# Two transformer blocks, first attention: low parts of fourteen gate panels on GpSimd instead of VectorE

## The chip, the cores and the metric

The kernel runs on one core of a Trainium2 chip. The metric is the device time of one execution in microseconds (us); lower is better. The core has TensorE (PE, matmuls, with its weight loads shown as PEld), VectorE (DVE), ScalarE (ACT), GpSimd (POOL) and the queue engine SyncE (SP). They run their own instruction streams and wait for each other through semaphores.

## The reference, cut to what matters

Two transformer blocks run one after the other on 512 tokens of width 1024, all in float32. The first begins with an attention of 8 "fox" heads and 8 "NSA" heads. Each NSA head is the sum of three softmax attentions: over compressed keys, selected keys and a window. Beside the attention, two gates of 1024 columns are made from the same normed input and weight the two attentions afterwards:

```python
h = rms_norm(x, g_attn)
z = h @ w_in                        # q, k, v, ..., g_a, g_b
s = q @ k^T * scale + bias          # per head; causal
p = softmax(s); o = p @ v
merged = sigmoid(g_a) * (o_fox @ w_br_fox) + sigmoid(g_b) * (o_nsa @ w_br_nsa)
x = x + merged @ w_out
```

The rest (a feed-forward part, then the second block with modulation, attention, a depthwise convolution and another feed-forward part) is untouched by the change.

## The kernel before, in words

**Panels.** Every weight matrix is cut into panels of 128x1024 numbers (512 KB). A panel goes through a ring of four slots: SP loads it into `raw`, ACT rounds it into `w_hi` (`panel_hi`, lines 666 to 670), VectorE subtracts `w_hi` from `raw` into `w_lo` (`panel_lo`, lines 1170 to 1175), and PE multiplies. A float32 product is three matmuls: high by high, high by low and low by high. Semaphores count in panel order: `hi_ready` and `lo_ready` say how many panels are split, `used` how many PE has finished. The split of a panel is made two panels ahead (`AHEAD = 2`).

**The attention.** It is a list of 32 steps, `inst`: 8 fox heads (steps 0 to 7), then for each of 8 NSA heads a compressed (cmp), a selected (slc) and a window (win) step. A step s of the PE stream (from line 2262 on) makes the scores of s (`qk`, line 2194), the transposed probabilities of step s-2 (`turn_p`, line 2214) and their product with the values (`pv`, lines 2239 and 2240). Between them it fills in matmuls of the 16 gate panels (`gate_fill`, lines 2253 to 2255), up to six places a step. Tables written out when the program is built (`GATE_FILL`, `GATE_ENDS`) say which gate piece goes where. The gate panels end in steps 1, 2, 4, 6, 8, 10, 12, 15, 17, 19, 21, 24, 26, 28, 30 and 33.

**VectorE in a step**, in this order: scores of step s with bias and row maximum (`score`, line 1340; t = 0 and 1, later 2 and 3), the sum of a head (`o_add`, 1394), the low parts of the transposed probabilities (`lo_turn`, 1378), the scaled gate output (`gate_out`, 1403), the softmax factor (1351, 1355) and the scaling of the probabilities of step s-1 (`normalize_tiles`, 1368, a tensor_scalar from and to SBUF). If a gate panel ended in this step, the low part of the panel two further on follows (`panel_lo`), and only then the low part of a finished head (`o_lo`, 1386) and the scores of the next step. PE's third score piece of a step waits for the first `score` of that step, and its transposes wait for the scaling.

**ScalarE in a step**: exponentials (763), high parts of transposed probabilities (774), `panel_hi` (669), the high part of a head (`o_hi`, 786), and for fox steps the four bias tiles of the next head (`fox_bias`, 755), for all of which the first score waits.

**GpSimd during the attention** issues transfers only. The loop at line 519 runs over 16 bias loads, n = 0 to 15: wait for the buffer (the fox bias of head n-2, or the scores of a later step), issue the bias transfer (533), and for n < 8 also wait for PE and issue the four key transfers of a head (`fox_keys`, 516) and one store of bias rows (537). Its other arithmetic comes later: squares of the context (547 to 553) and seven convolution taps (573 to 578).

Of the kernel before, what the change touches and what calls it, by code (L numbers as in the profile page):

```python
# [16 lines left out]
F32 = mybir.dt.float32  # L17
F32R = mybir.dt.float32r
ALU = mybir.AluOpType
# [27 lines left out]
RING = 4  # L47
AHEAD = 2
# [37 lines left out]
BASE, PANELS = {}, 0  # L86
# [6 lines left out]
def build(nc, a, out):  # L93
# [7 lines left out]
    def place(name, shape, dt, at=None):  # L101

        n = int(np.prod(shape[1:]))
        n = (n + 7) // 8 * 8
        if at is None:
            at = mark["at"]
            mark["at"] += n
        assert at + n <= room, (name, at, n, room)
        return nc.alloc_sbuf_tensor_at(name, list(shape), dt, offset=base0 + 4 * at)

    raw = place("raw", [P, RING, 8, P], F32)
    w_hi = place("w_hi", [P, RING, 8, P], F32R)
    w_lo = place("w_lo", [P, RING, 8, P], F32R, 0)
# [166 lines left out]
    def sem(name):  # L280
        if name not in sems:
            sems[name] = nc.alloc_semaphore(name)
        return sems[name]
# [3 lines left out]
    hi_ready = sem("panel_hi_ready")  # L287
    lo_ready = sem("panel_lo_ready")
# [35 lines left out]
    NI = len(inst)  # L324
# [84 lines left out]
    def gates_ended(s):  # L409
        return [g for (r, n), g in sorted(GATE_ENDS.items()) if r == s]  # L410
# [73 lines left out]
    def _(gp):  # L484
# [21 lines left out]
        def fox_keys(h):  # L506
# [7 lines left out]
            for m, k in enumerate((k_hi, k_lo)):  # L514
                for half in HALF:
                    gp.dma_start(kd[h % 2][half, m, :], k[HALF[h % 2], h // 2, :]).then_inc(sem(f"keys_loaded_{h % 2}"), 16)

        gp.wait_ge(sem("rows_stored"), 16)
        for n in range(16):
            if n == 8:  # L520
                gp.wait_ge(sem("rel_stored"), 16 * 8)
            if n >= 2:
                m = n - 2
                if m < 8:
                    gp.wait_ge(sem("fox_bias"), 4 * (m + 1))
                else:
                    gp.wait_ge(sem("scored"), 4 * (8 + 3 * (m - 8) + 3))
            if n < 8:
                src = bass.AP(tensor=scratch_c.tensor, offset=n * T, ap=[[0, P], [1, T]])
            else:  # L530
                head = (n - 8) // 2 + 4 * ((n - 8) % 2)
                src = bass.AP(tensor=scratch_r.tensor, offset=head * P * 640 + 127, ap=[[639, P], [1, T]])
            gp.dma_start(bias[:, n % 2, :], src).then_inc(sem(f"bias_loaded_{n % 2}"), 16)
            if n < 8:
                fox_keys(n)
                gp.wait_ge(sem("rel_rows"), 2)
                gp.dma_start(scratch_r[:, n * REL_ROWS:(n + 1) * REL_ROWS, :],
                             r8[:].unsqueeze(1).to_broadcast([8, REL_ROWS, 640])).then_inc(sem("rel_stored"), 16)
        gp.wait_ge(sem("qk_done"), NT * 8)
        gp.dma_start(cst[:, C_EARLY:C_ALL], a["consts"][:, C_EARLY:C_ALL]).then_inc(in_c2, 16)  # L540
        gp.wait_ge(used, done(BASE["branch"] + 7))
# [604 lines left out]
    def _(dve):  # L1146
# [24 lines left out]
        def panel_lo(n, also=0):  # L1171

            dve.wait_ge(hi_ready, n + 1)
            dve.tensor_tensor(w_lo[:, n % RING], raw[:, n % RING], w_hi[:, n % RING].bitcast(F32), ALU.subtract)\  # L1174
               .then_inc(lo_ready, 1 + also)
# [234 lines left out]
        for s in range(NI + 3):  # L1410
            score(s, 0)
            score(s, 1)
            if s >= 3 and head_end(s - 3):
                o_add(s - 3)
            lo_turn(s - 2, 0)
            gate_at(s, 0)
            score(s, 2)
            score(s, 3)
            if s == 0:
                proj_low("n3")  # L1420
                panel_lo(BASE["gate"] + 1)
            if s == 1:
                dve.wait_ge(sem("vc_hi_done"), 1)
                dve.tensor_tensor(vcs[:, :, 1, :], ps[0:CW, 7, P:2 * P].rearrange("p (g d) -> p g d", g=2),
                                  vcs[:, :, 0, :].bitcast(F32), ALU.subtract)\
                   .then_inc(sem("vc_lo_done"), 1)
            gate_at(s, 1)
            lo_turn(s - 2, 1)
            gate_at(s, 2)
            normalize_factor(s - 1)  # L1430
            lo_turn(s - 2, 2)
            gate_at(s, 3)
            normalize_tiles(s - 1, (0, 1))
            lo_turn(s - 2, 3)
            if s < NI + 2:
                gate_at(s, 4, 5)
            normalize_tiles(s - 1, (2, 3))
            for g in gates_ended(s) if s < NI + 2 else []:
                panel_lo(BASE["gate"] + g + AHEAD)
            if s >= 3 and head_end(s - 3):  # L1440
                o_lo(s - 3)
        for g in gates_ended(NI + 2):
            panel_lo(BASE["gate"] + g + AHEAD)
            gate_out(g)
        dve.wait_ge(bank_free, BASE["branch"] + 2)
# [156 lines left out]
        for c in range(4):  # L1602
            for m in range(8):
                n = BASE[f"ff1_{c}"] + m
# [10 lines left out]
            for m in range(8):  # L1615
                n = BASE[f"ff2_{c}"] + m
# [4 lines left out]
                if c == 0 and m == 0:  # L1621
                    g = vec[:, V_AT["g_final"]:V_AT["g_final"] + 8]
# [19 lines left out]
        for m in range(8):  # L1642
            n = BASE["ff2_3"] + m
# [303 lines left out]
        for c in range(3):  # L1947
            g = f"up_{c}"
# [710 lines left out]
```

## Time and profile before

| | before |
|---|---|
| median of 3 runs | 1712.98 us (1711.72 to 1714.76) |
| the profiled execution's own time | 1713.54 us |
| its span in the trace | 1711.8 us |
| busy: PE, DVE, ACT, POOL | 95%, 65%, 42%, 10% of the span |
| granted PE clock, mean | 0.986 of full speed |

The profiled execution is 0.56 us above the median, and 1.74 us of it lie outside the span. The attention with its gate panels fills some 165 us to 406 us of the span. A busy PE is not one at its peak: matmuls overlap, and their ends are modelled. In a row of the timeline the bracket says how long the engine was idle before it and who released it; "x4" means that four instructions of one kind are merged, with their common length.

### The profile page before, as it was taken

How to read it: one execution, taken by the hardware profiler on the slowest of the kernel's cores; microseconds unless marked ns; L12 is line 12 of the kernel's file. 1: busy time of each engine (PE TensorE's matmuls, PEld its weight loads, DVE VectorE, ACT ScalarE, POOL GpSimd, SP SyncE). 2: the span in 40 equal slices, each digit the busy share in tenths (PEclk: the TensorE clock that was granted, in tenths of full speed). 3: DMA queues.
4: the chain of work that ended last, by engine and by line, in shares of the span. 5: the costliest groups of instructions: out<-in, count | busy, mean ns of one | idle time of the engine just before them, and what ended most of it. 6: DMA issues, size and time to landing. Idle time of an engine off the chain costs nothing.

```text
span 1711.8 us, 21979 instructions
## 1 busy us (share of the span) xinstructions
PE 1629.8 (95%) x7956; PEld 1345.3 (79%) x7956; DVE 1110.3 (65%) x1700; ACT 716.3 (42%) x1232; POOL 164.7 (10%) x187
## 2 busy tenths in 40 slices
PE   7999889998999999999989999999899899999997
PEld 5877777776788888888867787888778888888886
DVE  6764787776577666663677479998665644444456
ACT  5353875555443232322443244444534432232233
POOL 0012400000120000000002980000000000000000
PEclk9999999999999999999999999999999999999999
DMA  4346921112535554531314221221232233332333
GB/s 160 120 123 175 190 69 50 46 49 61 219 113 178 203 202 168 207 135 63 98 37 136 87 73 44 63 62 50 92 123 76 86 98 98 94 92 97 99 98 99
DMA packets 49969, 185.43 MB, mean 108 GB/s; under 512 B 6928, under 2 KB 9232, under 8 KB 47456
## 3 DMA queue, kind: packets, MB, share of 16 engines
q1 hardware_dynamic: 39600, 136.76, 25.0%
q0 software_dynamic: 10288, 47.60, 9.8%
q8 instruction: 51, 0.84, 0.2%
q14 instruction: 30, 0.25, 0.0%
HBM read 172.23 MB, written 6.85 MB: 105 GB/s over the span
## 4 chain that ended last, share of the span: by engine, by line
PE 77%; DVE 12%; ACT 5%; issue 3%; DMA 2%; SPq 0%; ACTq 0%; DVEq 0%
PE ps L2004 17%; PE ps L2005 16%; PE ps L2006 16%; PE ps L2066 2%; PE ps L2067 2%; PE ps L2068 2%; ACT w_hi L669 1%; PE ps L2253 1%; PE ps L2214 1%; PE ps L2255 1%; PE ps L2421 1%; PE ps L2419 1%; PE ps L2254 1%; PE ps L2420 1%; DMA raw<-in_panels 1%
## 5 line engine op out<-in xcount | busy, mean ns | idle before, releaser
L2004 PE MATMUL ps<-h_hi,w_hi 128*128 128x512 f32 x832 | 329.2, 396 | 9.5 <-DVE h_lo L1672 3.7
L2005 PE MATMUL ps<-h_lo,w_hi 128*128 128x512 f32 x832 | 324.0, 389 | 0.0
L2006 PE MATMUL ps<-h_hi,w_lo 128*128 128x512 f32 x832 | 323.9, 389 | 0.0
L1174 DVE TENSOR_TENSOR w_lo<-raw,w_hi 128x1024 fp32r<-128x1024 f32 x181 | 228.4, 1264 | 119.0 <-ACT w_hi L669 93.0
L602 ACT ACTIVATE w_hi<-raw 128x1024 fp32r<-128x1024 f32 x125 | 131.4, 1052 | 168.3 <-DMA raw<-in_panels 162.3
L2004 PEld LDWEIGHTS ps<-h_hi,w_hi 128*128 128x128 f32 x832 | 156.2, 188 | 49.8 <-DVE h_lo L1672 5.8
L2005 PEld LDWEIGHTS ps<-h_lo,w_hi 128*128 128x128 f32 x832 | 156.2, 188 | 33.4 <-issue 1.9
L2006 PEld LDWEIGHTS ps<-h_hi,w_lo 128*128 128x128 f32 x832 | 156.2, 188 | 32.9
L2004 PE MATMUL ps<-f_hi,w_hi 128*128 128x512 f32 x408 | 164.8, 404 | 0.0
L2005 PE MATMUL ps<-f_lo,w_hi 128*128 128x512 f32 x408 | 159.1, 390 | 0.0
L2006 PE MATMUL ps<-f_hi,w_lo 128*128 128x512 f32 x408 | 159.0, 390 | 0.0
L669 ACT ACTIVATE w_hi<-raw 128x1024 fp32r<-128x1024 f32 x122 | 127.9, 1051 | 43.1 <-DMA raw<-in_panels 42.8
L2066 PE MATMUL ps<-h_hi,w_hi 128*128 128x512 f32 x184 | 75.4, 410 | 18.1 <-DVE w_lo L1174 18.1
L1159 DVE TENSOR_TENSOR w_lo<-raw,w_hi 128x1024 fp32r<-128x1024 f32 x70 | 85.6, 1223 | 8.5 <-DVE tmp_s L1959 4.5
L2006 PEld LDWEIGHTS ps<-f_hi,w_lo 128*128 128x128 f32 x408 | 76.6, 188 | 16.2
L2004 PEld LDWEIGHTS ps<-f_hi,w_hi 128*128 128x128 f32 x408 | 76.8, 188 | 13.8 <-issue 0.2
L2005 PEld LDWEIGHTS ps<-f_lo,w_hi 128*128 128x128 f32 x408 | 76.9, 188 | 13.6 <-issue 0.2
L774 ACT ACTIVATE pt_hi<-ps 128x512 fp32r<-128x512 f32 (+4 forms) x104 | 46.4, 447 | 72.5 <-PE ps L2214 71.8
L2067 PE MATMUL ps<-h_lo,w_hi 128*128 128x512 f32 x184 | 73.9, 402 | 0.0
L880 ACT ACTIVATE tmp_v<-tmp_s 128x512 f32<-128x512 f32 x32 | 20.2, 633 | 128.1 <-DVE tmp_s L1608 128.1
L1378 DVE TENSOR_TENSOR pt_lo<-ps,pt_hi 128x512 fp32r<-128x512 f32 (+4 forms) x104 | 52.4, 504 | 32.9 <-ACT pt_hi L774 30.6
L2068 PE MATMUL ps<-h_hi,w_lo 128*128 128x512 f32 x184 | 73.4, 399 | 0.0
(421 smaller groups left out, 3347.3 us busy)
## 6 DMA issues: line engine op xcount, KB each, us to landing
raw<-in_panels SPq DMA_DIRECT2D x252, 512.0 KB, 3.5
wm<-in_w_mod POOLq DMA_DIRECT2D x16, 1536.0 KB, 8.3
scratch_r<-r POOLq DMA_DIRECT2D x8, 320.0 KB, 10.6
bias<-scratch_c POOLq DMA_DIRECT2D x8, 256.0 KB, 10.4
kd<-k_hi POOLq DMA_DIRECT2D x16, 128.0 KB, 4.4
kd<-k_lo POOLq DMA_DIRECT2D x16, 128.0 KB, 6.8
bias<-scratch_r POOLq DMA_DIRECT2D x8, 256.0 KB, 3.1
X<-in_x POOLq DMA_DIRECT2D x1, 2048.0 KB, 9.7
```

The costliest lines, as they stand in the source:

```text
L602: act.activation(w_hi[:, slot], raw[:, slot], ACT.Copy).then_inc(hi_ready, 1)
L669: act.activation(w_hi[:, n % RING], raw[:, n % RING], ACT.Copy).then_inc(hi_ready, 1)
L774: act.activation(pt_hi[0:rows, at:at + w], ps[0:rows, 4 + r % 2, 0:w], ACT.Copy).then_inc(sem("pt_hi_done"), 1)
L1159: dve.tensor_tensor(w_lo[:, slot], raw[:, slot], w_hi[:, slot].bitcast(F32), ALU.subtract).then_inc(lo_ready, 1)
L1174: dve.tensor_tensor(w_lo[:, n % RING], raw[:, n % RING], w_hi[:, n % RING].bitcast(F32), ALU.subtract)\
L1378: dve.tensor_tensor(pt_lo[0:rows, at:at + w], ps[0:rows, 4 + r % 2, 0:w], pt_hi[0:rows, at:at + w].bitcast(F32), ALU.subtract).then_inc(se ...
L2004: pe.matmul(out, w_hi[:, u, b, :], hi[:, k, :N], start=start, stop=False)
L2005: pe.matmul(out, w_hi[:, u, b, :], lo[:, k, :N], start=False, stop=False)
L2006: ins = pe.matmul(out, w_lo[:, u, b, :], hi[:, k, :N], start=False, stop=stop)
L2066: pe.matmul(out, hi, h_hi[:, k, :], start=k == 0, stop=False, skip_group_check=True)
L2067: pe.matmul(out, hi, h_lo[:, k, :], start=False, stop=False, skip_group_check=True)
L2068: ins = pe.matmul(out, lo, h_hi[:, k, :], start=False, stop=k == KT - 1, skip_group_check=True)
```

## The change

GpSimd makes the low parts of gate panels 2 to 15, in its own stream, in place of VectorE. Before each bias load n it makes those panels whose gate ended before step `BIAS_STEP[n]`. That puts panel 2 before load 4, panel 3 before load 5, panel 4 before load 7, panel 5 before load 9, panel 6 before load 10, panels 7 and 8 before load 11, panel 9 before load 12, panel 10 before load 13, panels 11 and 12 before load 14, panel 13 before load 15, and panels 14 and 15 after load 15, ahead of the load of the rotary constants. VectorE keeps the panels around them and waits for GpSimd's count before the next one it makes itself.

```diff
+        def gate_low(g):
+
+            n = BASE["gate"] + g + AHEAD
+            gp.wait_ge(hi_ready, n + 1)
+            gp.wait_ge(lo_ready, n)
+            gp.tensor_tensor(w_lo[:, n % RING], raw[:, n % RING], w_hi[:, n % RING].bitcast(F32), ALU.subtract)\
+              .then_inc(lo_ready, 1)
+
+        BIAS_STEP = [n - 2 if n < 10 else 10 + 3 * (n - 10) for n in range(16)]
+        LOWS = [(s, g) for s in range(NI + 2) for g in gates_ended(s) if g + AHEAD < 16]
+
+        def gate_lows(until):
+
+            while LOWS and LOWS[0][0] < until:
+                gate_low(LOWS.pop(0)[1])
+
         gp.wait_ge(sem("rows_stored"), 16)
         for n in range(16):
+            gate_lows(BIAS_STEP[n])
...
+        gate_lows(NI + 2)
         gp.wait_ge(sem("qk_done"), NT * 8)
...
             for g in gates_ended(s) if s < NI + 2 else []:
-                panel_lo(BASE["gate"] + g + AHEAD)
+                if g + AHEAD >= 16:
+                    dve.wait_ge(lo_ready, BASE["gate"] + g + AHEAD)
+                    panel_lo(BASE["gate"] + g + AHEAD)
...
         for g in gates_ended(NI + 2):
+            dve.wait_ge(lo_ready, BASE["gate"] + g + AHEAD)
             panel_lo(BASE["gate"] + g + AHEAD)
```

## Rows read from the trace of the kernel before

**Rows 1.** The page: the chain by engine, and one kind of transfer with its landing time.

```profile
PE 77%; DVE 12%; ACT 5%; issue 3%; DMA 2%; SPq 0%; ACTq 0%; DVEq 0%
...
bias<-scratch_c POOLq DMA_DIRECT2D x8, 256.0 KB, 10.4
```

**Rows 2.** Windows, attention: length, busy PE, PEld, DVE, ACT, POOL, clock, DMA, GB/s.

```profile
165.00:390.00 225.00, 207.24 (x1113) 163.88 (x1113) 175.23 (x565) 150.83 (x426) 24.67 (x45) 0.97 0.36 84
```

**Rows 3.** Waits of PE, 165 to 390 us: total, times, longest.

```profile
PE ps L2194 <- DVE neg_max L1340: 3.6, 5, 0.9
```

**Rows 4.** Groups of DVE by line, 175 to 375 us: the moved instruction.

```profile
L1174 DVE TENSOR_TENSOR w_lo<-raw,w_hi 128x1024 fp32r<-128x1024 f32 x14 | 17.1, 1219 | 2.6 <-ACT w_hi L669 2.6
```

**Rows 5.** Timeline of steps 5, 9 and 13: start, length, instruction, idle before.

```profile
205.05 1.21 DVE L1174 TENSOR_TENSOR w_lo<-raw,w_hi 128x1024 fp32r<-128x1024 f32 x1
...
207.27 0.29 DVE L1340 CUSTOM_DVE_ANT_0 sb<-ps,sb 128x128 f32<-128x128 f32 x1 [0.28 <-ACT sb L755]
...
237.76 1.22 DVE L1174 TENSOR_TENSOR w_lo<-raw,w_hi 128x1024 fp32r<-128x1024 f32 x1
...
239.01 0.69 DVE L1386 TENSOR_TENSOR qs<-o_sum,qs 64x512 fp32r<-64x512 f32 x1
...
240.08 0.45 PE L2194 MATMUL ps<-kn_hi,nqs 128*128 128x384 f32 x1 [0.55 <-DVE neg_max L1340]
...
266.22 1.23 DVE L1174 TENSOR_TENSOR w_lo<-raw,w_hi 128x1024 fp32r<-128x1024 f32 x1 [0.66 <-ACT w_hi L669]
...
267.12 0.60 PE L2211 MATMUL ps<-cst,p_cmp 128*32 128x128 f32 x4
267.71 0.44 PE L2194 MATMUL ps<-kn_hi,nqs 128*128 128x384 f32 x1
```

**Rows 6.** Instructions of lines 547 and 578: shortest, median, longest in ns.

```profile
L547 POOL TENSOR_TENSOR c_sq<-x_ctx x8: 607/839/1595, 465.6 to 481.2; 128x256 f32<-128x256 f32 x8
L547 POOLq MODIFY_POOL_CONFIG  x2: 42/42/42, 454.3 to 454.3; - x2
...
L578 POOL TENSOR_TENSOR conv<-conv,conv_p x24: 1267/1292/1988, 934.7 to 1019.0; 128x512 f32<-128x512 f32 x24
```

**Rows 7.** Timeline of POOL and DVE where both compute, later in the kernel.

```profile
467.69 0.61 POOL L547 TENSOR_TENSOR c_sq<-x_ctx 128x256 f32<-128x256 f32 x1
467.98 0.60 DVE L1467 COPY sq_acc<-tmp_s 128x512 f32<-128x512 f32 x1
...
968.32 1.29 POOL L578 TENSOR_TENSOR conv<-conv,conv_p 128x512 f32<-128x512 f32 x1
968.45 2.23 DVE L1174 TENSOR_TENSOR w_lo<-raw,w_hi 128x1024 fp32r<-128x1024 f32 x1 [4.69 <-ACT w_hi L669]
```

**Rows 8.** Instructions of line 1485: the same copy with GpSimd quiet.

```profile
L1485 DVE COPY sq_acc<-tmp_s x2: 417/417/417, 1293.7 to 1672.9; 128x512 f32<-128x512 f32 x2
```

**Rows 9.** Timeline around the scaling (L1368) of steps 2, 10 and 28.

```profile
187.03 1.05 ACT L669 ACTIVATE w_hi<-raw 128x1024 fp32r<-128x1024 f32 x1
...
188.50 0.81 DVE L1368 TENSOR_SCALAR sb<-sb,factor 128x384 f32<-128x384 f32 x2
...
250.23 0.54 POOL L533 DMA_DIRECT2D bias<-scratch_r  x1 [25.26 <-DVE neg_max L1340]
...
250.85 1.27 DVE L1368 TENSOR_SCALAR sb<-sb,factor 128x128 f32<-128x128 f32 x4
...
252.18 0.66 PE L2214 MATMUL ps<-cst,sb 128*128 128x128 f32 x4 [0.58 <-DVE sb L1368]
...
368.89 1.04 ACT L669 ACTIVATE w_hi<-raw 128x1024 fp32r<-128x1024 f32 x1
...
370.40 1.27 DVE L1368 TENSOR_SCALAR sb<-sb,factor 128x128 f32<-128x128 f32 x4
```

**Rows 10.** Timeline: bias load 4 is issued, and ScalarE begins to use it.

```profile
180.82 0.57 POOL L533 DMA_DIRECT2D bias<-scratch_c  x1 [1.24 <-ACT sb L755]
...
196.26 1.91 ACT L755 ACTIVATE sb<-bias,c_q 128x128 f32<-128x128 f32 x4
```

## The prediction

> **What bounds the kernel now.** I read the page first, then the stages, then the waits, then single steps. The chain on the page is 77% PE and 12% DVE [rows 1]: the kernel is bound by TensorE, and VectorE matters only where PE waits for it. In the stretch of the attention where the fourteen moved instructions lie, PE is busy for 207.2 of 225 us and VectorE for 175.2, with GpSimd at 24.7 [rows 2]. So no more than about 18 us of PE idle time can be had there, from whatever cause. The moved work is fourteen subtractions of 1.219 us, 17.1 us in all [rows 4]. That is not the gain. The gain is only what PE waits right behind them, and the wait in question is that of the third score piece for the first score: 3.6 us in five cases [rows 3], one of which (step 1) belongs to a panel that VectorE keeps.
>
> **What is removed.** I went through the places one by one.
> - Steps 5 and 7 (fox). The w_lo begins at 205.05 and ends at 206.26, yet the first score starts at 207.27 and was released by ScalarE's bias tiles, after 0.28 us of idleness [rows 5]. Without w_lo it starts at the same time. Gain: nothing.
> - Step 9. After w_lo comes the head's low part (0.69 us) and then the score, and PE has 0.55 us of idle time in front of its score piece [rows 5]. This would come back, if nothing took its place.
> - Four steps like 13 (the others are 16, 22 and 25). VectorE waits 0.66 us for w_hi and works 1.23 us, then scores. PE starts four transposes at 267.12 and the next score piece only at 267.71, right as the first score (some 0.28 us, behind w_lo) must end [rows 5]. No bracket marks a wait, but part of these 0.59 us is one: bounds nothing and 0.59, and I take 0.35. Gain: 4 x 0.35 = 1.4 us.
> - In the remaining places (steps 2, 11, 18, 20, 27, 29) PE does not wait behind w_lo.
>
> **What is added: the length on GpSimd.** The trace has no 128x1024 tensor_tensor on POOL. A 128x256 one takes at least 0.607 us and a 128x512 one 1.267 us, median 1.292 [rows 6]. Another 512 columns at the same slope give an estimate of 1.29 + 2 x 0.68 = 2.65 us. Bounds: 2.4 us (four times the smallest) and 4.0 us (twice the slowest 512-column one). I take 2.65. As to PE this is hidden: a low part is made one whole gate panel ahead, ten or more us, so PE will not wait for it. VectorE's new wait for the count before the two panels it keeps (steps 31 and 33) costs nothing for the same reason: the last moved panel belongs to step 28.
>
> **What is added: the two engines get in each other's way.** This is the term that decides. At 967 to 971 us a w_lo that takes 1.22 us alone takes 2.23 us; it began at 968.45 under a POOL tensor_tensor that ended at 969.61 [rows 7, 4]. The 1.01 us extra are the rest of that instruction (1.16) less 0.15. A copy from SBUF to SBUF takes 0.417 us alone and 0.602 us when it begins 0.32 us before the end of a POOL instruction [rows 7, 8]: again the rest, less 0.14. So a VectorE instruction of either kind simply stands until GpSimd's is over. The page "SBUF — State Buffer" of the Trainium skill has this as a rule (section "Who interferes with whom"): a VectorE instruction with two SBUF inputs, or in a mode that uses two ports, fully blocks against a GpSimd instruction that reads SBUF, whoever starts second. The trace agrees, with the two cases above.
>
> What is caught during 2.65 us after w_hi is done?
> - Step 3 (w_hi of step 2). It is done at 188.08; the scaling (two instructions, 0.81 us) starts at 188.50 [rows 9]. It would be held until 188.08 + 2.65 - 0.14 = 190.6 and end at 191.4, against 189.3. The score came after w_lo, at 190.4; now at 191.4. PE waits for both. Cost +1.0 us.
> - Steps 5 and 7. GpSimd gets the port when the scaling ends, by 205.05, and holds it to 207.7. The head's low part (two SBUF inputs, 0.69 us) is then held to 207.55 and ends at 208.25, where the score used to start at 207.27 [rows 5]. +1.0 us each, 2.0.
> - Step 9. From 237.76 to 240.4; the low part ends at 240.95 and not at 239.70 [rows 5]. +1.25 us, instead of the gain of 0.55.
> - Step 29. w_hi is done at 369.93, 0.47 us before the four scalings at 370.40 [rows 9]; GpSimd has nothing else to do. They are held for 2.65 - 0.47 - 0.14 = 2.0 us, and PE's transposes wait for them (as in step 11, 0.58 us already [rows 9]). +2.0 us.
> - Steps 11 and 20, the same pattern, but here GpSimd is issuing a bias transfer until 250.77, and the scaling starts at 250.85 [rows 9]. Which comes first can't be told from 0.08 us. If GpSimd: 2.65 - 0.08 - 0.14 = 2.4 us each. If VectorE: nothing, as its work goes back to back. I count half, 2.4 us for the two.
> - Steps 2, 13, 16, 18, 22, 25 and 27: behind w_hi come scores and low parts with one operand in PSUM. Nothing is caught; in 18 and 27 only if GpSimd slips in between two scalings.
>
> **GpSimd's own queue.** Behind each subtraction stands a bias load. Load 4 is issued at 180.82, lands 10.4 us later and is first used at 196.26 [rows 1, 10]: 5.0 us of room, of which the subtraction takes at most 1.5 to 2. The later loads are further ahead. The load of the rotary constants moves behind panel 15; it is used in the second block. Cost nothing. If this cover went, ScalarE's bias tiles would be late, then the first score, then PE.
>
> **The sum.** -1.4 + 1.0 + 2.0 + 1.25 + 2.0 + 2.4 = +7.25 us. The profiled execution took 1713.54, so 1720.8; its median stands 0.56 lower, so 1720.2. Nothing downstream gives it back: after the attention PE is the bound again, and panels are loaded as PE uses them.
>
> **Rivals.**
> 1. The blocking is as weak for these forms as if it weren't there. For it speaks that no row shows a tensor_scalar beside a POOL tensor_tensor; against it the copy. Then step 9 and the four like 13 gain 0.55 + 1.4 = 2.0 us, and 0.4 in step 3: 2.4 us, 1710.6. It decides once the instructions of steps 3, 5, 7 and 9 are held for less than about 0.5 us each instead of some 2. With every wait behind the first scores gone (3.6 us of rows 3 and 1.4) it would be at most 5 us, 1708.
> 2. Part of the cost is absorbed: VectorE has 17 us less to do, and where PE is held for the scaling, later waits of the step shrink. With steps 11 and 20 won by VectorE and a quarter of the rest absorbed: 0.75 x 4.85 = +3.6, 1716.6.
> 3. GpSimd's first arithmetic must be set up. MODIFY_POOL_CONFIG comes at 454.3 and the first tensor_tensor at 465.6, behind a transfer that covers the gap [rows 6], so its price lies between nothing and 11.3 us. It would now come ahead of panel 2, and with GpSimd free 1.24 us before 180.82 [rows 10] load 4 would land at 179.6 + 11.3 + 2.65 + 10.4 = 204.0, which is 7.7 us late; step 3's collision (1.0) would be avoided. That gives up to 6.7 us more, 1726.9. The page "GPSIMD Engine Reference" (section "Instruction dispatch") puts a first load at some 6 us; by this estimate load 4 would be 2.4 us late and the time 1721.6. No run here shows it.
> 4. A clock drop. PE's granted clock is 0.97 over the stage [rows 2]; longer stalls might add a stretch at 1.2 GHz or take one away, some 2 us either way. This widens the range only.
>
> **How the numbers follow.** Forecast (blocking, sum between 4.85 and 9.65 us) 0.58; rival 1, 0.13; rival 2, 0.16; rival 3, 0.13. A measurement of this kernel can tell about 0.2%, 3.4 us. Faster by more needs rival 1 at its end: 0.06. Within 3.4 us: the rest of rival 1 and half of rival 2, 0.17. Slower: 0.77. The range reaches from 1711.5 (rival 1 short of its centre) to 1727 (rival 3 at its bound, or the full sum with drops).
>
> **What would show it.** Right: fourteen POOL subtractions near 2.65 us; L1368 and L1386 rows longer by up to 2.5 us in steps 2 to 10, 19 and 28; longer waits of L2214 and L2194; no change in slc and win steps but a small gain. Wrong: L1368 and L1386 at their old lengths; PE waiting for w_lo; ScalarE's L755 waiting for a bias transfer.

## The result, and the profile after

The changed kernel takes 1730.25 us (median of 5 runs, 1727.54 to 1731.13) against 1713.3 for the kernel before (5 runs): ratio 1.0097, 95% interval 1.0083 to 1.011. It is slower, by more than twice what I had forecast (1720.2), and it lies above my range, which ended at 1727. The profiled execution took 1731.13 us.

In the changed file the lines have moved: the scaling is L1386 (before L1368), the head's low part L1404 (L1386), the product that makes the scaling's factors L1373 (L1355), the scores L1358 (L1340), the transposes of PE L2235 (L2214), its score pieces L2215 (L2194), VectorE's w_lo L1192 (L1174). The subtractions on GpSimd are L523, the bias loads L550.

The page of the changed kernel: span, busy time, chain by engine, the bias loads.

```profile
span 1729.3 us, 21995 instructions
...
PE 1634.3 (95%) x7956; PEld 1349.0 (78%) x7956; DVE 1116.1 (65%) x1686; ACT 716.3 (41%) x1232; POOL 198.6 (11%) x201
...
PE 75%; DVE 14%; ACT 5%; issue 4%; DMA 2%; SPq 0%; ACTq 0%; DVEq 0%
...
bias<-scratch_c POOLq DMA_DIRECT2D x8, 256.0 KB, 9.2
```

The chain gave two per cent from PE to VectorE [rows 1 for before]. The bias loads land in 9.2 us, not later than before (10.4), so by this figure nothing in that queue suffered. Now PE's waits for the whole attention, changed kernel, 167 to 407 us: total, times, longest.

```profile
PE ps L2235 <- DVE sb L1386: 14.3, 8, 2.9
...
PE ps L2215 <- DVE neg_max L1358: 4.1, 4, 1.6
```

The wait of rows 3 (3.6 us, for the first scores) is still there, though w_lo is gone from before them; it now comes with the held low part of steps 5 and 7, as below at 212.91. Beside it stands one that is much larger: PE's transposes wait for the scaling, 14.3 us in eight cases. The same view of the kernel before, 165 to 390 us, has it at its old size:

```profile
PE ps L2214 <- DVE sb L1368: 2.4, 4, 0.7
```

The subtractions themselves, line 523: shortest, median, longest in ns, first and last start.

```profile
L523 POOL TENSOR_TENSOR w_lo<-raw,w_hi x14: 2349/2398/2660, 181.1 to 382.9; 128x1024 fp32r<-128x1024 f32 x14
L523 POOLq MODIFY_POOL_CONFIG  x2: 74/74/74, 180.9 to 181.0; - x2
```

They take 2.40 us, my lower bound, where I took 2.65. The configuration takes 74 ns and the first subtraction begins at 181.05, right behind it.

The timeline of the changed kernel around four collisions, in steps 3, 5, 9 and 11: start, length, instruction, idle time before.

```profile
190.40 2.35 POOL L523 TENSOR_TENSOR w_lo<-raw,w_hi 128x1024 fp32r<-128x1024 f32 x1 [1.19 <-ACT w_hi L687]
190.74 2.62 DVE L1386 TENSOR_SCALAR sb<-sb,factor 128x384 f32<-128x384 f32 x2
193.41 1.11 PE L2235 MATMUL ps<-cst,sb 128*128 128x128 f32 x4 [2.46 <-DVE sb L1386]
...
209.32 2.66 POOL L523 TENSOR_TENSOR w_lo<-raw,w_hi 128x1024 fp32r<-128x1024 f32 x1 [1.05 <-ACT w_hi L687]
209.93 2.60 DVE L1404 TENSOR_TENSOR qs<-o_sum,qs 64x512 fp32r<-64x512 f32 x1 [0.19 <-ACT qs L804]
212.91 0.44 PE L2215 MATMUL ps<-kd,qs 128*128 128x384 f32 x1 [1.55 <-DVE neg_max L1358]
...
242.95 2.95 DVE L1386 TENSOR_SCALAR sb<-sb,factor 128x384 f32<-128x384 f32 x2
243.24 2.37 POOL L523 TENSOR_TENSOR w_lo<-raw,w_hi 128x1024 fp32r<-128x1024 f32 x1 [12.99 <-ACT w_hi L687]
...
257.57 2.54 DVE L1373 TENSOR_TENSOR factor<-factor,gate_t 128x4 f32<-128x4 f32 x1
257.71 2.37 POOL L523 TENSOR_TENSOR w_lo<-raw,w_hi 128x1024 fp32r<-128x1024 f32 x1
260.15 1.27 DVE L1386 TENSOR_SCALAR sb<-sb,factor 128x128 f32<-128x128 f32 x4
261.48 1.10 PE L2235 MATMUL ps<-cst,sb 128*128 128x128 f32 x4 [2.94 <-DVE sb L1386]
```

Read each pair together. At 190.74 two scalings that take 0.81 us take 2.62, until 0.6 us after the subtraction ends. At 209.93 the head's low part (0.69 us alone) takes 2.60. So far this is what I had described. At 242.95 the first of two scalings had already begun when GpSimd came, and the pair still took 2.95 us: GpSimd got in between the two (the second one, 128x512, begins at 243.28 and takes 2.62 us). And at 257.57 it is not the scaling that is held but the product before it, four numbers wide, which takes 0.166 us in the kernel before (next row). Its record begins 0.14 us before that of the subtraction.

```profile
L1355 DVE TENSOR_TENSOR factor<-factor,gate_t x24: 165/166/171, 243.4 to 395.1; 128x4 f32<-128x4 f32 x24
```

In step 2 the lead is longer still. The last scaling of that step, seen by itself (180.6 to 182 us, one engine at a time):

```profile
180.44 3.35 DVE L1386 TENSOR_SCALAR sb<-sb,factor 128x512 f32<-128x512 f32 x1
...
181.05 2.44 POOL L523 TENSOR_TENSOR w_lo<-raw,w_hi 128x1024 fp32r<-128x1024 f32 x1
```

Alone it takes 0.47 us, so it would have ended at 180.91, 0.14 us before the subtraction's record begins. It did not.

The clock is the second part. Windows of the kernel before and then of the changed one: stretch, length, busy PE, PEld, DVE, ACT, POOL, granted clock, DMA share, GB/s.

```profile
165.00:195.00 30.00, 26.08 (x147) 21.48 (x148) 20.12 (x59) 21.57 (x52) 12.36 (x24) 1.00 0.94 192
...
370.00:400.00 30.00, 27.06 (x136) 20.66 (x137) 22.46 (x73) 17.04 (x51) 0.00 (x0) 0.94 0.11 35
```

```profile
165.00:195.00 30.00, 23.73 (x131) 19.28 (x130) 21.22 (x51) 20.73 (x49) 15.35 (x21) 0.97 0.95 196
...
370.00:400.00 30.00, 26.04 (x136) 21.02 (x134) 22.18 (x67) 13.92 (x44) 4.64 (x3) 0.89 0.13 38
```

PE's clock falls to its lower level, 1.2 GHz, at 193.3, as the long wait of step 3 ends, and at 384.4, within the one that ends at 386.6. Before, it did not fall in step 3, and in step 29 it was low for 3.4 us where it now is for 6.8.

### The profile page after: what moved, and what is told of

Read it like the earlier page. It is cut to its first block, busy times and chain, and to the rows that moved or that the text cites. A ratio compares the mean times of both kernels' runs of the same rounds, so it can differ in the third digit from the quotient of the medians.

```text
span 1729.3 us, 21995 instructions
## 1 busy us (share of the span) xinstructions
PE 1634.3 (95%) x7956; PEld 1349.0 (78%) x7956; DVE 1116.1 (65%) x1686; ACT 716.3 (41%) x1232; POOL 198.6 (11%) x201
## 4 chain that ended last, share of the span: by engine, by line
PE 75%; DVE 14%; ACT 5%; issue 4%; DMA 2%; SPq 0%; ACTq 0%; DVEq 0%
PE ps L2025 17%; PE ps L2027 16%; PE ps L2026 16%; PE ps L2087 2%; PE ps L2089 2%; PE ps L2088 2%; PE ps L2235 2%; ACT w_hi L687 1%; PE ps L2274 1%; DMA raw<-in_panels 1%; PE ps L2275 1%; PE ps L2276 1%; PE ps L2440 1%; PE ps L2442 1%; PE ps L2441 1%
## 5 line engine op out<-in xcount | busy, mean ns | idle before, releaser
L1192 DVE TENSOR_TENSOR w_lo<-raw,w_hi 128x1024 fp32r<-128x1024 f32 x167 | 210.5, 1263 | 114.7 <-ACT w_hi L687 90.2
L1177 DVE TENSOR_TENSOR w_lo<-raw,w_hi 128x1024 fp32r<-128x1024 f32 x70 | 85.6, 1223 | 8.5 <-DVE tmp_s L1980 4.5
L898 ACT ACTIVATE tmp_v<-tmp_s 128x512 f32<-128x512 f32 x32 | 20.2, 633 | 128.6 <-DVE tmp_s L1629 128.6
```

Source lines behind the costliest of these rows:

```text
L1177: dve.tensor_tensor(w_lo[:, slot], raw[:, slot], w_hi[:, slot].bitcast(F32), ALU.subtract).then_inc(lo_ready, 1)
```

## The experiments

**How the steps are compared.** The length of an attention step is the time from PE's first score piece of one step to that of the next. The attention (all steps, up to the first product behind it) takes 241.21 us in the kernel before and 255.35 in the changed one, 14.14 more. The spans differ by 17.5; the other 3.4 us lie before the attention (1.5) and behind it (1.9), where nothing was changed. The table gives the length of each step less its length before, in us. Steps 13, 16, 22 and 25 stand as one sum, as do the steps right behind them (14, 17, 23 and 26); steps that are left out moved by 0.06 or less. The last column is PE's time at 1.2 GHz within the attention, found by stepping short windows through it; for the kernel before it is 13.6. A drop that begins while PE already waits for the first product behind the attention is not counted.

| kernel | 2 | 3 | 5 | 7 | 9 | 11 | 18 | 20 | 27 | 29 | 31 | 13.. | 14.. | attention | at 1.2 GHz |
|---|---|---|---|---|---|---|---|---|---|---|---|---|---|---|---|
| changed | 0.75 | 2.36 | 0.66 | 0.65 | 0.99 | 2.39 | 1.16 | 2.24 | 1.13 | 2.59 | 0.15 | -1.05 | 0.05 | 255.35 | 20.4 |
| e7_again | 0.74 | 2.23 | 0.67 | 0.65 | 1.01 | 3.79 | 1.15 | 1.59 | 1.12 | 2.02 | 0.12 | -1.09 | 0.08 | 255.35 | 20.4 |
| e1_none | 0.00 | -0.43 | -0.02 | -0.01 | -0.84 | -1.00 | 0.02 | -2.30 | -0.01 | -1.01 | 0.16 | -1.10 | 0.05 | 234.77 | 0 |
| e2_late | -0.01 | -0.46 | 0.00 | 0.00 | -0.85 | -0.91 | 0.01 | 0.02 | -0.02 | -0.91 | 0.13 | -1.01 | -0.02 | 237.11 | 6.8 |
| e2b_late | 0.00 | -0.44 | -0.03 | -0.02 | -0.81 | -0.94 | 0.01 | -2.21 | 0.00 | -0.91 | 0.15 | -1.00 | -0.01 | 235.06 | 0 |
| e9_late_all | -0.01 | -0.44 | -0.01 | -0.02 | -0.82 | -0.93 | 0.01 | -2.21 | -0.04 | -0.91 | -0.49 | -1.17 | 0.15 | 234.45 | 0 |
| e5_cmp | 0.00 | 0.00 | -0.03 | -0.03 | 0.01 | 3.42 | -0.01 | 1.59 | -0.03 | 2.02 | 0.15 | 0.33 | 0.02 | 248.62 | 17.0 |
| e4_win | 0.00 | -0.02 | -0.03 | 0.00 | 0.00 | 0.08 | 0.01 | -1.31 | 0.00 | 1.40 | 0.15 | -1.08 | 0.10 | 240.45 | 13.6 |
| e3_pieces | 0.00 | -0.27 | -0.01 | 2.90 | -0.22 | 2.97 | -0.02 | 1.63 | -0.02 | 2.34 | 0.13 | -1.07 | 0.04 | 249.60 | 23.8 |
| e12_gaps | 0.00 | -0.28 | -0.02 | -0.03 | -0.24 | 3.27 | 0.00 | 1.75 | 0.01 | 2.76 | 0.14 | -0.95 | 0.07 | 247.61 | 20.4 |
| e6_write | -0.03 | -0.42 | -0.01 | -0.02 | -0.36 | 0.46 | 0.00 | 0.69 | 0.01 | 0.22 | 0.15 | -1.00 | -0.03 | 240.99 | 13.6 |
| e10_normed | 0.00 | -0.43 | 2.54 | 0.97 | -0.82 | -1.01 | -0.01 | 0.06 | -0.01 | -1.01 | 0.15 | -1.03 | 0.03 | 240.72 | 10.2 |
| e8_dve_late | -0.01 | -0.32 | 0.09 | 0.11 | -0.35 | -0.16 | 0.00 | -0.85 | 0.01 | -0.13 | 0.25 | -1.09 | 2.08 | 240.93 | 3.4 |

### 1. The subtraction is not made at all (e1_none)

```diff
-            gp.tensor_tensor(w_lo[:, n % RING], ...).then_inc(lo_ready, 1)
+            gp.sem_inc(lo_ready, 1)
...
-            hi, lo = w_hi[:, n % RING, k, :], w_lo[:, n % RING, k, :]
+            hi, lo = w_hi[:, n % RING, k, :], (w_lo if g < 2 else w_hi)[:, n % RING, k, :]
```

> Neither engine makes the low parts of gate panels 2 to 15; GpSimd only counts them ready, and TensorE takes the high part in their place (same matmuls, other numbers). VectorE is relieved as in the changed kernel, and GpSimd's port use is gone. Theory A (port blocking: VectorE stands still while GpSimd's subtraction runs) expects the whole loss gone and the small gain left: 1710 to 1713 us, ratio 0.997 to 1.000, and every scaling and head low part at its length of before. Rival B (GpSimd's later bias and key transfers, or the moved load of the rotary constants, hold up ScalarE and TensorE) expects the loss to shrink by the 2.4 us per panel of queue time only, and the same if something outside the attention changed. Rival C (the new counts and waits themselves, which stay) expects the loss to stay, about 1728.

Measured: 1709.5 us, ratio 0.9966 (0.9952 to 0.998). The attention takes 234.77 us, 20.6 less than in the changed kernel, and PE runs at full clock through all of it. Every loss of the changed kernel is gone, and steps 9, 11, 20 and 29 are shorter than before. So the loss comes from the subtraction while it runs, not from GpSimd's waits or the order of its stream. And 6.4 us under the kernel before is what this stage gives when VectorE is freed of this work and nothing is held; the most of it comes through the clock, as experiment 2 shows.

### 2. The same work, begun later (e2_late, and again as e2b_late)

GpSimd waits, before each subtraction, until VectorE has made the first score of the next step. Nothing else is changed; all fourteen subtractions are made.

```diff
-        def gate_low(g):
+        def gate_low(g, s):
...
             gp.wait_ge(lo_ready, n)
+            gp.wait_ge(sem("scored"), NT * (s + 1) + 1)
             gp.tensor_tensor(w_lo[:, n % RING], ...
```

> The changed kernel with one more wait: GpSimd starts a low part only when the first score of the next step has been made, so behind the scaling and the head's low part. Same work, same engine, some 1 to 4 us later, so bias loads 4, 5 and 7 go out up to 3 us later. Theory A expects the blocking to fall on nothing (scores and the low parts of probabilities have one operand in PSUM): 1710 to 1714 us, ratio 0.998 to 1.001. Rival B (queue order) expects no better than 1730, rather worse, since the transfers are later still. Theory A is also wrong if scores (L1358) or low parts (L1396) get longer here.

> The kernel with the later start again, in more rounds and beside the next three. If the gain over the kernel before is real: ratio 0.996 to 0.9985.

Measured: 1710.77 us, ratio 0.9968 (0.9951 to 0.9984), and 1708.68, 0.9965 (0.9952 to 0.9978). The two intervals agree: this version beats both the kernel before and the changed one. Its attention is 235.06 us, 0.3 above that with no subtraction at all. The timeline of e2b_late in step 11 (product L1375, scaling L1388, score L1360, low part of the probabilities L1398):

```profile
249.48 0.17 DVE L1375 TENSOR_TENSOR factor<-factor,gate_t 128x4 f32<-128x4 f32 x1
...
249.68 1.27 DVE L1388 TENSOR_SCALAR sb<-sb,factor 128x128 f32<-128x128 f32 x4
...
252.38 0.69 DVE L1398 TENSOR_TENSOR pt_lo<-ps,pt_hi 128x512 fp32r<-128x512 f32 x1
...
252.51 2.39 POOL L524 TENSOR_TENSOR w_lo<-raw,w_hi 128x1024 fp32r<-128x1024 f32 x1 [2.92 <-DVE neg_max L1360]
```

The product is back at 0.17 us, and the subtraction lies under scores and a low part whose first operand is in PSUM; the latter keeps its 0.69 us. PE's waits in e2b_late, 165 to 390 us:

```profile
PE ps L2237 <- DVE sb L1388: 2.6, 5, 0.7
PE ps L2217 <- DVE neg_max L1360: 2.6, 4, 0.9
```

The wait for the scaling is at its old size. The pair of profiles also prices the clock: one and the same kernel had 6.8 us at 1.2 GHz in e2_late and none in e2b_late, and its attention was 2.05 us longer, nearly all of it in step 20: 0.30 us for each. This is an estimate from one pair, and in the same step a product is held a little too (0.58 us in e2_late, 0.27 in e2b_late, for 0.17 alone). The window around that stretch, e2_late and then e2b_late, same columns as above:

```profile
310.00:335.00 25.00, 24.55 (x123) 19.60 (x123) 17.04 (x65) 14.45 (x43) 5.32 (x3) 0.87 0.14 40
```

```profile
310.00:335.00 25.00, 24.35 (x133) 18.67 (x132) 18.29 (x73) 14.81 (x48) 5.34 (x3) 1.00 0.10 32
```

PE is busy for the same time in both (24.55 and 24.35 us); in the first the trace has 123 of its instructions in the window, in the second 133.

### 3. Four shorter subtractions (e3_pieces)

```diff
+            for q in range(4):
+                b = slice(2 * q, 2 * q + 2)
+                ins = gp.tensor_tensor(w_lo[:, n % RING, b], raw[:, n % RING, b], ...)
+            ins.then_inc(lo_ready, 1)
```

> The changed kernel with each subtraction in four pieces of 128x256, some 0.6 us each, at the same place. Theory A in the form of the prediction (an instruction waits for the rest of one GpSimd instruction) expects each blocked VectorE instruction to lose at most 0.6 us and so the loss to fall from 17 us to about 4 to 8 us: 1717 to 1721. If GpSimd's next piece takes the port again before VectorE's waiting instruction gets it, the loss stays: 1728 to 1732.

Measured: 1723.48 us, ratio 1.0044 (1.0027 to 1.0061). The time lies between the two that I had expected, since each of the two outcomes holds for some of the steps. The pieces remove the loss of steps 2, 3, 5, 9, 18 and 27 and keep, or enlarge, that of 7, 11, 20 and 29. The timeline shows both cases, first step 5, then steps 7 and 11 (head's low part L1406):

```profile
205.63 3.53 POOL L525 TENSOR_TENSOR w_lo<-raw,w_hi 128x256 fp32r<-128x256 f32 x4 [1.20 <-ACT w_hi L689]
206.23 0.96 DVE L1406 TENSOR_TENSOR qs<-o_sum,qs 64x512 fp32r<-64x512 f32 x1 [0.18 <-ACT qs L806]
...
223.04 2.79 POOL L525 TENSOR_TENSOR w_lo<-raw,w_hi 128x256 fp32r<-128x256 f32 x4
223.11 3.28 DVE L1406 TENSOR_TENSOR qs<-o_sum,qs 64x512 fp32r<-64x512 f32 x1 [0.20 <-ACT qs L806]
...
254.23 2.94 DVE L1375 TENSOR_TENSOR factor<-factor,gate_t 128x4 f32<-128x4 f32 x1
254.36 2.78 POOL L525 TENSOR_TENSOR w_lo<-raw,w_hi 128x256 fp32r<-128x256 f32 x4
```

At 205.63 the pieces had first to wait for VectorE (3.53 us for the four, against 2.79), and then VectorE's low part was held for the rest of one piece only. At 223.04 and 254.36 the pieces ran back to back, and VectorE's instruction stood through all four: 3.28 us against 2.58 in step 7 of the changed kernel, and 2.94 against 2.54 in step 11. The product of step 20 stands through all four as well (2.95 us). Everywhere else VectorE gets in after one piece; in step 29 that does not help, for its product takes 0.56 us but the next pieces then hold its four scalings (2.66 us instead of 1.27). So cutting an instruction up does not by itself let the other engine in. What decides between the two cases these runs do not settle.

### 4. Pieces with a gap between them (e12_gaps)

Each of the pieces of experiment 3 is followed by a wait for its own end, so that the next is not yet in the queue.

```diff
+                if q < 3:
+                    ins.then_inc(sem("low_piece"), 1)
+                    gp.wait_ge(sem("low_piece"), 3 * (n - BASE["gate"] - AHEAD) + q + 1)
```

> The four pieces of 128x256 again, but GpSimd waits for the end of each piece before it issues the next. In the four-piece kernel without these waits VectorE's tiny factor product (0.17 us alone) took 2.94 us in step 11, longer than any single piece (0.6 to 0.75 us): it stood through all of them. If GpSimd keeps the port because its next instruction is already queued, then a gap lets VectorE in, each held instruction loses at most about 0.7 us, and the loss falls from 1.0044 to 1.000 to 1.002 although GpSimd is busy longer. If the port always goes back to GpSimd first, the factor products still take 2.5 us or more and the ratio stays at 1.004 or above.

Measured: 1720.01 us, ratio 1.0042 (1.0028 to 1.0057). Step 11 again (product L1378, scaling L1391):

```profile
250.22 0.92 DVE L1378 TENSOR_TENSOR factor<-factor,gate_t 128x4 f32<-128x4 f32 x1
...
250.35 3.28 POOL L525 TENSOR_TENSOR w_lo<-raw,w_hi 128x256 fp32r<-128x256 f32 x4
251.17 2.74 DVE L1391 TENSOR_SCALAR sb<-sb,factor 128x128 f32<-128x128 f32 x4
```

The product now takes 0.92 us, not 2.94: VectorE does get in at the gap. But the next piece then catches its next instructions, and the four scalings take 2.74 us instead of 1.27. Step 11 is 3.27 us longer all the same. In step 7, where the head's low part stands alone, the gap does help: it takes 0.96 us and the step is as long as before, where the four pieces without gaps cost 2.90 us. So neither of my two outcomes came: the products are short and the ratio stays. A gap helps only an engine that has just one thing to do in it.

### 5. Three places alone (e5_cmp)

Only the low parts behind steps 10, 19 and 28 go to GpSimd, VectorE makes the others.

```diff
-        LOWS = [(s, g) for s in range(NI + 2) for g in gates_ended(s) if g + AHEAD < 16]
+        LOWS = [(s, g) for s in range(NI + 2) for g in gates_ended(s) if s in (10, 19, 28)]
...
-                if g + AHEAD >= 16:
+                if s not in (10, 19, 28):
```

> Only the three low parts behind steps 10, 19 and 28 are on GpSimd; VectorE makes the other eleven as before. In the changed kernel the steps after them were longer by 2.39, 2.24 and 2.59 us. Theory A expects the costs to add up place by place: +7.2 us, 1720.5 us, ratio 1.004. If the loss comes from something common to the whole stage (clock, queue, load of GpSimd's code) it should be either nearly all there or nearly nothing.

Measured: 1722.58 us, ratio 1.0044 (1.0028 to 1.0061). Steps 11, 20 and 29 are 3.42, 1.59 and 2.02 us longer, 7.03 in all, and the other steps are nearly as before (0.15 in step 31, 0.33 in the four like 13 together). In all three it is the factor product that was caught (2.63, 2.54 and 2.19 us). In step 11 some 1 us of the 3.42 is the clock (3.4 us more at 1.2 GHz). In step 20 only 1.59 of the 2.37 us for which the product is held come through; PE waits there until 316.89, and its clock is low from 314.6 to 321.4 us, so a third of the drop now falls into the wait, which fits but was not tested by itself. Three instructions of fourteen carry half of the attention's loss, and the loss belongs to the place, not to the number of subtractions.

### 6. Four places alone (e4_win)

As experiment 5, with steps 12, 15, 21 and 24 (those whose low part stood ahead of the four gains in my sum).

> Only the four low parts that end in compressed and window steps with nothing but scores behind them (ended in steps 12, 15, 21 and 24) are on GpSimd. Theory A expects the small gain of these places alone, 0.2 to 0.3 us in each of steps 13, 16, 22 and 25 and no loss anywhere: 1.0 us, ratio 0.999 to 1.0005, which the times can't tell from none; the trace can.

Measured: 1712.59 us, ratio 0.999 (0.998 to 0.9999), so near to 1 that the steps have to show it. The four steps are shorter by 0.27, 0.22, 0.31 and 0.28, 1.08 in all. The rest (-1.31 in step 20, +1.40 in step 29) comes from the clock, whose 13.6 us at 1.2 GHz lie elsewhere: 3.4 of them have moved from step 20 to step 29.

### 7. A fill in place of the subtraction (e6_write)

GpSimd writes zeros over the low part, so it writes SBUF and reads nothing. The low parts of these panels are then zero.

```diff
-            gp.tensor_tensor(w_lo[:, n % RING], raw[:, n % RING], ..., ALU.subtract).then_inc(lo_ready, 1)
+            gp.memset(w_lo[:, n % RING].bitcast(F32), 0.0).then_inc(lo_ready, 1)
```

> At the place of each of the fourteen subtractions GpSimd fills the tile with zeros instead: it writes SBUF and reads nothing, so the low parts of gate panels 2 to 15 are zero. It tells apart which VectorE instructions are held by what. By reads alone (theory A1): neither the head's low part (L1404) nor the scaling (L1386) is held, and the time is as in the kernel with no low parts, 1709 to 1712. By either port (theory A2): the scaling, which writes at two elements a cycle, stands until the fill ends, and the head's low part and the small factor product do not: steps 3, 9, 18 and 27 are longer by up to the length of the fill, steps 5, 7, 11, 20 and 29 are not, 1711 to 1716.

Measured: 1710.63 us, ratio 0.9981 (0.9972 to 0.999). Step 11, then step 29 (product L1372, scaling L1385), and the row of all products:

```profile
250.27 0.17 DVE L1372 TENSOR_TENSOR factor<-factor,gate_t 128x4 f32<-128x4 f32 x1
...
250.38 0.97 POOL L523 MEMSET w_lo<- 128x1024 f32 x1
250.48 1.81 DVE L1385 TENSOR_SCALAR sb<-sb,factor 128x128 f32<-128x128 f32 x4
...
369.79 0.95 POOL L523 MEMSET w_lo<- 128x1024 f32 x1 [11.31 <-ACT w_hi L686]
...
370.00 0.17 DVE L1372 TENSOR_TENSOR factor<-factor,gate_t 128x4 f32<-128x4 f32 x1
```

```profile
L1372 DVE TENSOR_TENSOR factor<-factor,gate_t x24: 164/166/168, 243.0 to 395.3; 128x4 f32<-128x4 f32 x24
```

The product, with two SBUF inputs, is not held by a fill: 168 ns is its longest. The clean case is that of step 29, where it lies wholly under the fill; in steps 11 and 20 it overlaps one by 0.06 us. The head's low part never meets a fill (the fill of step 5 ends at 205.65, the low part begins at 205.96), so this run says nothing of it. The scaling, with one input, is held: 1.81 us for the four instead of 1.27. I had expected steps 3, 9, 18 and 27 to be longer and steps 11, 20 and 29 not. It came the other way round: the first four are as before or shorter, and the last three are 0.46, 0.69 and 0.22 us longer, since the scaling starts under the fill there. This is what the Trainium skill's page "SBUF — State Buffer" states in "Who interferes with whom": two SBUF inputs clash with a GpSimd instruction that reads, not with one that only writes, and forms that use two ports clash with any. The trace agrees with both halves, with the first by the product alone.

### 8. A wait for the end of the scaling (e10_normed)

```diff
             gp.wait_ge(lo_ready, n)
+            gp.wait_ge(sem("normed"), s)
```

> GpSimd starts each low part when VectorE has finished the scaling of that step, and so ahead of the head's low part and the first scores. Theory A expects: steps 2, 3, 11, 18, 20, 27 and 29 lose nothing (the scaling is never held), steps 5 and 7 are 0.7 us longer than before as in the changed kernel, step 9 about 0.5 to 1 us longer (the head's low part held for some 2.4 us), and the clock drops of steps 11 to 29 are those of the kernel before or fewer: 1710 to 1715 us, ratio 0.998 to 1.001. If something other than the held instructions made steps 3, 11, 20 and 29 long, they stay 2.2 to 2.6 us longer.

Measured: 1713.79 us, ratio 0.9986 (0.9977 to 0.9995). All that hung on the scaling and its product is gone (steps 2, 3, 11, 18, 27 and 29), and steps 5 and 7, where the head's low part comes right behind the scaling, pay (0.97 in step 7; 2.54 in step 5, with a drop of the clock behind it). The timeline in steps 5 and 9:

```profile
205.12 2.37 POOL L524 TENSOR_TENSOR w_lo<-raw,w_hi 128x1024 fp32r<-128x1024 f32 x1 [1.62 <-DVE sb L1388]
205.13 2.90 DVE L1406 TENSOR_TENSOR qs<-o_sum,qs 64x512 fp32r<-64x512 f32 x1 [0.19 <-ACT qs L806]
...
241.26 0.69 DVE L1406 TENSOR_TENSOR qs<-o_sum,qs 64x512 fp32r<-64x512 f32 x1
...
241.35 2.86 POOL L524 TENSOR_TENSOR w_lo<-raw,w_hi 128x1024 fp32r<-128x1024 f32 x1 [13.93 <-DVE sb L1388]
```

In step 5 both want the port within 0.01 us and VectorE is held, its 0.69 us becoming 2.90; in step 9 VectorE is first by 0.09 us and GpSimd is held, 2.86 us instead of 2.37, which costs nothing: the step is 0.82 shorter. I had expected steps 5 and 7 to lose 0.7 us each and step 9 to be 0.5 to 1 us longer; the first two lost more, and step 9 gained. The same two instructions cost or save the time by who comes first.

### 9. VectorE alone, later (e8_dve_late)

The kernel before, with VectorE making the low part behind the first two scores of the next step; GpSimd makes none.

```diff
             score(s, 0)
             score(s, 1)
+            for g in gates_ended(s - 1) if s < NI + 3 else []:
+                panel_lo(BASE["gate"] + g + AHEAD)
```

> The kernel before with nothing on GpSimd: VectorE still makes all low parts, but each one behind the first two scores of the next step instead of ahead of them (the last one, too). If the gain of the later start comes from freeing the place ahead of the first score, this gives most of it without a second engine: 1710 to 1713 us, ratio 0.997 to 0.999. If it comes from the 17 us taken off VectorE, or if the w_lo now delays the low parts of the probabilities, it gives nothing or a loss: 1.000 to 1.003.

Measured: 1715.76 us, ratio 1.0004 (0.9994 to 1.0015), no change. The gains of steps 3, 9 and 13 and its like appear, but steps 14, 17, 23 and 26 give back 0.5 us each: now the low part of the probabilities comes behind w_lo. In steps 11 and 29 the clock no longer falls either, yet they are only 0.16 and 0.13 us shorter, where experiment 2 has 0.9 (e2b_late); what takes the rest there was not looked into. So the gain of experiment 2 needs both, the other engine and the later start.

### 10. Later, and with the last two panels (e9_late_all)

Experiment 2, with panels 16 and 17 on GpSimd too.

> The later start, and panels 16 and 17 on GpSimd as well. Panel 17's low part (1.23 us on VectorE) stands ahead of the last head's sum, on the path to the branch product: 0.7 us better than the later start alone if VectorE was what the sum waited for there, 1.5 us worse if GpSimd's 2.4 us hold the last head's low part (two operands in SBUF). I expect 0.5 to 0.7 us better, which the times alone can't tell; the trace can.

Measured: 1708.9 us, ratio 0.997 (0.996 to 0.998). Step 31 is 0.64 us shorter than in e2b_late and the attention takes 234.45 us, the shortest of all. In the whole time this can't be told from experiment 2.

### 11. The changed kernel again (e7_again)

> The changed kernel once more, beside the next two, to see how much of its 17 us is the attention stage. In the first profile the attention was 14.1 us longer, the part before it 1.5 us (it differs by up to 2.2 us between kernels that are the same there) and the part after it 1.9 us. Theory A gives the kernel 14 us and expects a ratio of 1.008 to 1.0095 here; if the rest of the kernel has really become slower, 1.0100 or more.

Measured: 1727.19 us against 1714.39, ratio 1.0071 (1.0058 to 1.0085), a little under what I had expected. The attention takes 255.35 us again, to the hundredth, and the table shows the same steps; only the clock's share moved, from steps 20 and 29 into 11. Outside the attention this profile is 1.6 us shorter than the kernel before, where the first was 3.4 longer. So the attention's 14.1 us are the change's doing, and the rest of the first comparison is not. The part of it behind the attention (1.9 us) goes with the clock: behind the attention PE's clock is low for 30.6 us in the first profile, 25.2 in the kernel before and 20.2 here, and that stretch takes 1307.2, 1305.2 and 1303.6 us. The part ahead of the attention (1.5 us) is absent here; the attention begins at 164.7 to 165.8 us in ten of the profiles and at 166.5 to 167.3 in four (the changed kernel, e2_late, e3_pieces, e9_late_all), and why stays open.

## Why the prediction was wrong

The direction and the mechanism were right, the size was not: 14.1 us in the attention, where the sum said 7.25. The whole kernel was 17.0 us slower in the first comparison and 12.8 in the second. By the steps of the sum:

- **"A VectorE instruction simply stands until GpSimd's is over"**: right, to the size. The product held at 257.57 ends at 260.11 after 0.17 us of work, so it got the port at 259.94, 0.14 before the subtraction's end at 260.08, the figure I had read from rows 7 and 8. Experiments 1 and 2 show that this is the cause, and experiment 7 that it goes by what the GpSimd instruction reads and writes and not by its running alone. What is not borne out is "whoever starts second": by the records the product of step 11 starts 0.14 us ahead of the subtraction, the last scaling of step 2 0.61 us ahead, and both are held.
- **Steps 11 and 20, "which comes first can't be told; I count half"**: the step that failed first, and 2.3 us of the miss. I looked at the scaling alone and left out the product ahead of it, which I had not listed among what can be caught. It begins 0.2 us earlier, and it has two SBUF inputs. GpSimd's record begins at 257.71, before the scaling's turn, and it caught the product in both steps: held for 2.37 us each, 4.7 in all instead of 2.4. There was no race to count half.
- **"VectorE's work goes back to back"**, from which steps 2, 18 and 27 were counted at nothing and step 9 at the head's low part: wrong. GpSimd gets in between two scalings in steps 9 (at 242.95), 18 and 27, and in step 2 the last scaling is held. Steps 2, 18 and 27 cost 0.75, 1.16 and 1.13, some 3.0 us that the sum had at zero. I had named the possibility for 18 and 27 and given it no price. In step 9 the scaling was held instead of the low part; its cost of 0.99 was near my 1.25 for another reason.
- **Steps 5 and 7**: 0.66 and 0.65 instead of 1.0 each. The subtraction's length was mis-sized: 2.40 us and not 2.65, which takes 0.25 off. The rest is its start: it ends 2.64 us into step 5 (209.34 to 211.98), where the forecast had 2.96 (204.74 to 207.7).
- **Step 29**: 2.0 forecast; the product was held for 2.19 - 0.17 = 2.02, and e5_cmp and e7_again have the step 2.02 longer. The agreement is in part luck, since I had named the scalings, from another start and with another length. **Step 3**: 1.0 forecast; of 2.36 about 1.23 is the held scaling, the rest the clock.
- **The four gains of 0.35**: 1.05 us measured instead of 1.4, confirmed by experiment 6 alone.
- **The clock, "this widens the range only"**: 20.4 us at 1.2 GHz instead of 13.6. At 0.30 us for each (the estimate of experiment 2) that is 2.0 us. I had seen that long stalls could do this and did not put it in the sum, though the forecast itself lengthened them.

Put right, the sum is 0.75 + 1.23 + 1.31 + 0.99 + 2.29 (steps 18 and 27) + 6.76 (steps 11, 20, 29) - 1.05 = 12.3, and 2.0 for the clock, 14.3; measured 14.1. Of the 7.1 us that my sum lacked, steps 11 and 20 are 2.3, steps 2, 18 and 27 are 3.0 and the clock 2.0; the other terms nearly cancel.

**The rivals.** The first (blocking as good as absent, 1710.6) fell with the first held row. What it described, VectorE freed and nothing held, exists in the kernel with the later start, at 1708.7; the gain there is larger than its 2.4 us because PE's clock no longer drops: 13.6 us at 1.2 GHz fewer than before, 4.1 us by the price above, of the 6.15 us that e2b_late's attention is shorter. They lie where the drops had been: steps 11, 20 and 29 are 0.9, 2.2 and 0.9 us shorter. In e2_late, where the clock falls in step 20 as before, that step is as long as before. So these gains are the clock's, and no run speaks against my reading that PE does not wait behind w_lo there. The second (steps 11 and 20 won by VectorE, a quarter of the rest absorbed) fell with steps 11 and 20. Absorption there is, though: in steps 11 and 29 the held time comes through in full, but in steps 2, 9, 18 and 27 VectorE is held for over 2 us each, and with w_lo gone from behind the steps are only 0.75 to 1.16 us longer. The third (a first setup of GpSimd) fell by the row of line 523: 74 ns, and bias loads that land in 9.2 us. The Trainium skill's page "GPSIMD Engine Reference" gives some 6 us for a first call ("Instruction dispatch"); no such gap is seen here, the subtraction starting at 181.05 behind the configuration of 180.9 to 181.0. The fourth, the clock, happened.

## What to carry to other kernels

Before arithmetic is moved to GpSimd, list every VectorE instruction that can come while it runs, the smallest too: what matters is not its length but its inputs and who waits for it. A four-element product on the critical path cost as much as the whole subtraction. Then choose when the work starts: tied to an event after which VectorE's work has an operand in PSUM, the same fourteen subtractions gave 0.9965 instead of 1.0097 (1.0071 in the second comparison). Look at the end of the work too: there a product was still held for up to 0.4 us (0.58 us for 0.17 in e2_late).

## What was not expected of the hardware

- GpSimd takes the port between two VectorE instructions that follow each other without a gap (242.95: 2.95 us for 0.81 us of work). The other way round it depends: in e3_pieces VectorE did not get in between GpSimd's queued pieces in steps 7, 11 and 20 (3.28, 2.94 and 2.95 us under four pieces), and did in the others (0.96 us in step 5).
- A VectorE instruction can be held although its record begins first: the 0.17 us product started 0.14 us before the subtraction and took 2.54 us, and the 0.47 us scaling of step 2 started 0.61 us before it and took 3.35. In e1_none, with the same transfer issued by GpSimd beside it and no subtraction behind, that scaling takes 0.47 us. In e6_write a scaling of 0.45 us that begins 0.87 us before the first fill takes 2.09. So GpSimd seems to hold VectorE from before its own record begins, at its first arithmetic instruction above all; why is open, and who comes first can't be read from the records alone. In e10_normed a lead of 0.09 us was enough for VectorE.
- Little decides over the clock. The waits of PE differ by about 1 us in all between the kernel before (3.6 us for the first scores, 2.4 for the scaling) and e2b_late (2.6 and 2.6), and PE's work is the same; yet its time at 1.2 GHz in this stage went from 13.6 us to none, or to 6.8 in e2_late, the same kernel.
